# Second attention: score products of 128 rows, and the probabilities' low part right behind the logits

## The chip, the cores and the metric

The kernel runs on one core of a Trainium2 chip. The metric is the device time of one launch in microseconds (us). A profiled execution is read beside it: its span runs from the first to the last instruction. Engines: TensorE (PE, and PEld for its weight loads), VectorE (DVE), ScalarE (ACT), GpSimd (POOL), SyncE (SP, here the queue of the weight transfers).

## The reference

A bidirectional encoder trunk of two layers on 512 tokens of 1024 features, all float32. Layer 0 mixes tokens by 2-D neighbourhood attention, layer 1 by sliding-window attention; each is followed by a squared-ReLU MLP, each part is preceded by an RMS norm, and one closes the trunk. The change lies in layer 1's attention:

```python
def sliding_window_gqa(h, w_qkv, sinks, rel_table, w_o):
    # 16 query heads of 64, 4 key/value heads; window |i-j| <= 128, in blocks of 128 tokens
    s = jnp.einsum('bnqhgd,bnjhd->bhgnqj', q, kb).astype(jnp.float32)
    ...
    s = jnp.where(jnp.asarray(mask), s + bias, jnp.finfo(jnp.float32).min)
    m = jnp.maximum(jnp.max(s, axis=-1, keepdims=True), sink)
    p = jnp.exp(s - m)
    p = p / (jnp.sum(p, axis=-1, keepdims=True) + jnp.exp(sink - m))
    o = jnp.einsum('bhgnqj,bnjhd->bnqhgd', p.astype(v.dtype), vb).reshape(B, S, D)
    return jnp.einsum('bsd,de->bse', o, w_o)
```

q is scaled by 1/8 (64 to the power -1/2), kb and vb are the keys and values of the three neighbouring blocks.

## The kernel before

Every operand of a matmul is held in two parts of a short format (fp32r): a high part, which ScalarE rounds off, and a low part, the rest, which VectorE gets by a subtraction. A product a x b is then three matmuls, high x high, low x high and high x low (`product`, L398; lines L400 to L402 of the profile). The weights come as 180 chunks of 128x1024, one transfer of 512 KB each, issued by SyncE when the chunk before is split; ScalarE makes w_hi (L802) and VectorE w_lo (L1086).

All engines run queues of their own, written out by hand in program order, and meet at semaphores. Nothing reorders them: an instruction that waits holds up all that is behind it on its engine.

The second attention runs over eight pairs of heads, p = 0 to 7, each with four blocks of 128 queries, n = 0 to 3. A block of one pair is called a unit here. Blocks 0 and 3 see two key blocks (256 columns), blocks 1 and 2 see three (384); so the two heads of a unit have 4 or 6 tiles of 128x128 probabilities (512 or 768 columns). A unit goes through this chain:

- TensorE `sw_scores` (L692, products at L504): for each of the two heads a contraction over its 64 features. Head 0 has its features in partitions 0 to 63 and head 1 in 64 to 127, so `head_products` (L498) issues high x high, high x low and low x high in pairs of 64-row matmuls, six in all. They go to one PSUM tile, s_ps, which is free again when the logits are made.
- VectorE `sw_logits` (L1364, L1178): adds the bias, negates and takes the minimum, one custom instruction a head.
- ScalarE `sw_exp` (L991, L864): exponential and row sum, one a head.
- TensorE `sw_transpose` (L701, L708): the 4 or 6 tiles, into pt_ps.
- ScalarE `pt_high` (L867, L869), VectorE `pt_low` (L1133, L1135): the two parts of the transposed probabilities, pt_parts.
- TensorE `sw_values` (L712; L534, L538): the weighted values, into one of two banks of om_ps, one for blocks 0 and 1 (g = 0), one for blocks 2 and 3 (g = 1).
- VectorE `sw_o_sum` (L1381, with L1386, L1389, L1143, L1145): adds the parts and divides, once for two blocks. TensorE `transpose_o` (L544, L547) transposes the result, ScalarE `sw_o_high` (L1013, L1015) and VectorE `sw_o_low` (L1397, L1399) split it.

`sw_step` exists on each engine and covers one pair: four positions n. TensorE's position n holds: the transposes of unit n-1, one dense part (three products of 512 columns for the next pair's queries, or in the last two steps for the output projection), the scores of unit n+1, another dense part, the values of unit n-1. The dense parts make the next query tile: VectorE scales it (`scale_queries`, L1115), ScalarE rounds it (`tile_high`, L856) and VectorE makes its low part (`queries_low`, L1125). One weight chunk a step is split too. The full steps are pairs 1 to 6; the step of pair 0 has no outputs before it, the step of pair 7 no queries behind it.

ScalarE's position n holds: the first exponential of unit n, [an output's high part], the transposed probabilities' high part of unit n-1, the second exponential of n, and what else is due. VectorE's position n holds: the logits of unit n, then outputs and queries where due, then the low part of unit n-1.

Of the kernel before, what the change touches and what calls it, by code (L numbers as in the profile page):

```python
# [19 lines left out]
ALU = mybir.AluOpType  # L20
ACT = mybir.ActivationFunctionType

P = 128
# [76 lines left out]
def encoder(nc, xT, wstream, gains, rpb, sinks, rel_table, na_mask, onehot, out):  # L100
# [3 lines left out]
    with ExitStack() as ctx:  # L104
# [71 lines left out]
        x_prepared, h_split, sq_cleared = sem("x_prepared"), sem("h_split"), sem("sq_cleared")  # L176
        idle_made, h_low, first_hi = sem("idle_made"), sem("h_low"), sem("first_hi")
# [61 lines left out]
        na_probs = probs[:, 0:QT * ROWS * WC].rearrange("p (j n) -> p j n", j=QT)  # L239

# [60 lines left out]
        def _(pool):  # L301
# [83 lines left out]
            split_weights(CH_MLP0 + 2)  # L385
            with pool.Fori(1, PAIRS // 2) as i:
# [10 lines left out]
        def _(pe):  # L397
# [294 lines left out]
            def sw_scores(p, n):  # L692

                if n == 0:
                    pe.wait_ge(tile_split, (p + (TI_SW + 3)).v)
                pe.wait_ge(logits_made, sw_unit(p, n).v)
                kb, nb = SW_BLOCKS[n]
                head_products(lambda hh: s_ps[:, hh, 0:nb * P], (8 + p.odd, slice(P * n, P * (n + 1))),
                              (p.odd, slice(P * kb, P * (kb + nb)))).then_inc(scores_done, 1)
# [29 lines left out]
            def sw_step(m, before=True, last=None):  # L729
# [59 lines left out]
            early_part(CH_SWO, GR_SWO, HEADS, 12, 16)  # L789
# [6 lines left out]
        def _(act):  # L796
# [50 lines left out]
            def tile_high(g, e, dst, square=None, order=None):  # L847
# [8 lines left out]
                nc.scalar.copy(dst, src).then_inc(tile_hi, 1)  # L856

# [202 lines left out]
            tile_high(At(GR_SW), At(TI_SW), k_hi[:, 0, :])  # L1060
            split_weights(At(CH_SW + 3))
            split_weights(At(CH_SW + 4))
            tile_high(At(GR_SW + 2), At(TI_SW + 1), k_hi[:, 1, :])
# [3 lines left out]
            tile_high(At(GR_SW + 4), At(TI_SW + 2), u_hi[:, 8, :])  # L1067
# [523 lines left out]
```

## Time and profile before

| | us |
|---|---|
| median of 3 runs (1148.69 to 1149.16) | 1148.82 |
| profiled execution | 1148.75 |
| its span | 1147.1 |
| TensorE busy | 1136.0 (99%) |
| VectorE busy | 630.4 (55%) |
| ScalarE busy | 504.8 (44%) |
| GpSimd busy | 138.0 (12%) |

The second attention, from its first scores (623) to its last values (753), takes 130 us of the span. A matmul's row in a timeline gives its start and a modelled time until its result is through; matmuls are pipelined, so the difference between two starts is what one costs, and the time in the second column is longer than that. For the other engines too the next instruction can start a little before the one ahead has ended. "[0.28 <-DVE nmax L1178]" behind a row means that its engine was idle for 0.28 us ahead of it, until VectorE's instruction of that line and tile released it. "x6" is a number of instructions merged into a row.

### The profile page before, as it was taken

The numbers are of one execution on the slowest core, as the hardware profiler recorded it, in microseconds if no ns is written. First come the engines' busy times: TensorE is split into PE (matmuls) and PEld (weight loads), VectorE is DVE, ScalarE is ACT, GpSimd is POOL, SyncE is SP. The second block draws the span as 40 slices with busy tenths as digits, with TensorE's granted clock in tenths as the row PEclk, the third lists the DMA queues.
The fourth block names the chain that finished last, engine by engine and source line by source line (L and its number), as shares of the span: only waits on it lengthen the run. The fifth ranks groups of instructions, "written<-read, shape, count | busy, mean of one in ns | idle before, by whom it ended". The sixth has DMA issues, their size and how long they took to land.

```text
span 1147.1 us, 16682 instructions
## 1 busy us (share of the span) xinstructions
PE 1136.0 (99%) x5644; PEld 937.1 (82%) x5644; DVE 630.4 (55%) x1020; ACT 504.8 (44%) x908; POOL 138.0 (12%) x239
## 2 busy tenths in 40 slices
PE   9999999999999999999999999999999999999997
PEld 6888888888888888888887788888888888888886
DVE  7788887764442234444345778766444223444333
ACT  6777677553431223333334666645343122333221
POOL 6544341330000000000000322100000000000000
PEclk9999999999999999999999999999999999999998
DMA  6322331343223222322222212123322332232222
GB/s 225 97 89 92 91 91 55 96 120 105 91 92 102 100 91 92 107 94 90 93 91 92 51 53 59 52 74 95 107 91 92 100 102 92 91 107 95 91 92 92
DMA packets 34291, 106.98 MB, mean 93 GB/s; under 512 B 5760, under 2 KB 8096, under 8 KB 34256
## 3 DMA queue, kind: packets, MB, share of 16 engines
q1 hardware_dynamic: 29344, 98.61, 26.2%
q0 software_dynamic: 4768, 7.90, 2.9%
q8 instruction: 21, 0.34, 0.1%
q14 instruction: 14, 0.11, 0.0%
q10 hardware_dynamic: 144, 0.02, 0.0%
HBM read 103.84 MB, written 2.67 MB: 93 GB/s over the span
## 4 chain that ended last, share of the span: by engine, by line
PE 98%; DVE 1%; DMA 0%; ACT 0%; SPq 0%; issue 0%; DVEq 0%; ACTq 0%
PE acc L400 29%; PE acc L402 28%; PE acc L401 28%; PE s_ps L504 3%; PE om_ps L538 2%; PE pt_ps L708 2%; PE om_ps L562 1%; PE om_ps L534 1%; PE pt_ps L525 1%; PE om_ps L494 1%; PE s_ps L400 1%; PE s_ps L401 1%; PE s_ps L402 1%; DMA w_raw<-in_wstream 0%; PE om_ps L547 0%; DVE x_res L1304 0%
## 5 line engine op out<-in xcount | busy, mean ns | idle before, releaser
L802 ACT CAST w_hi<-w_raw 128x1024 fp32r<-128x1024 f32 x179 | 188.1, 1051 | 401.5 <-PE acc L402 395.1
L400 PE MATMUL acc<-h_hi,w_hi 128*128 128x512 f32 x792 | 318.4, 402 | 0.7 <-DVE w_lo L1086 0.7
L401 PE MATMUL acc<-h_lo,w_hi 128*128 128x512 f32 x792 | 308.9, 390 | 0.0
L402 PE MATMUL acc<-h_hi,w_lo 128*128 128x512 f32 x792 | 308.8, 390 | 0.0
L1086 DVE TENSOR_TENSOR w_lo<-w_raw,w_hi 128x1024 fp32r<-128x1024 f32 x177 | 217.9, 1231 | 143.7 <-ACT w_hi L802 143.0
L400 PE MATMUL acc<-u_hi,w_hi 128*128 128x512 f32 (+1 forms) x624 | 241.2, 387 | 0.0
L401 PE MATMUL acc<-u_lo,w_hi 128*128 128x512 f32 (+1 forms) x624 | 239.5, 384 | 0.0
L402 PE MATMUL acc<-u_hi,w_lo 128*128 128x512 f32 (+1 forms) x624 | 239.5, 384 | 0.0
L400 PEld LDWEIGHTS acc<-h_hi,w_hi 128*128 128x128 f32 x792 | 148.8, 188 | 37.5 <-issue 4.8
L402 PEld LDWEIGHTS acc<-h_hi,w_lo 128*128 128x128 f32 x792 | 148.7, 188 | 31.7
L401 PEld LDWEIGHTS acc<-h_lo,w_hi 128*128 128x128 f32 x792 | 149.1, 188 | 28.5 <-issue 0.7
L1115 DVE SCALAR_TENSOR_TENSOR scaled<-acc,rstd 128x512 f32<-128x512 f32 x90 | 61.9, 689 | 143.9 <-PE acc L402 142.4
L400 PEld LDWEIGHTS acc<-u_hi,w_hi 128*128 128x128 f32 x624 | 117.2, 188 | 24.1 <-issue 0.5
L402 PEld LDWEIGHTS acc<-u_hi,w_lo 128*128 128x128 f32 x624 | 117.2, 188 | 23.2
L401 PEld LDWEIGHTS acc<-u_lo,w_hi 128*128 128x128 f32 x624 | 117.3, 188 | 22.6
L348 POOL DMA_DIRECT2D bias_pairs<-t_shifted x64 | 32.8, 575 | 448.9 <-ACT esink L1007 428.4
L864 ACT ACTIVATE probs<-probs,nmax 128x256 f32<-128x256 f32 (+1 forms) x128 | 67.9, 532 | 35.3 <-DVE nmax L1178 35.3
L1260 DVE TENSOR_TENSOR x_res<-acc,x_res 128x512 f32 (+1 forms) x39 | 26.9, 690 | 99.5 <-PE acc L402 99.5
L1125 DVE TENSOR_TENSOR u_lo<-scaled,u_hi 128x512 f32 (+1 forms) x80 | 59.1, 738 | 13.9 <-ACT u_hi L856 13.9
L331 POOL TENSOR_TENSOR bias_masked<-bias_pairs,mask 128x256 f32<-128x256 f32 x64 | 52.3, 857 | 83.2 <-DVE nmax L1178 81.2
L856 ACT CAST u_hi<-scaled 128x512 f32 (+1 forms) x80 | 49.7, 621 | 7.2
L1135 DVE TENSOR_TENSOR pt_parts<-pt_ps,pt_parts 128x1024 fp32r<-128x1024 f32 (+2 forms) x48 | 45.8, 955 | 10.5 <-ACT pt_parts L869 10.3
(141 smaller groups left out, 1000.1 us busy)
## 6 DMA issues: line engine op xcount, KB each, us to landing
w_raw<-in_wstream SPq DMA_DIRECT2D x180, 512.0 KB, 3.3
bias_pairs<-rpb_reversed POOLq DMA_DIRECT2D x64, 62.0 KB, 2.4
bias_pairs<-t_shifted POOLq DMA_DIRECT2D x64, 48.0 KB, 2.2
x_res<-in_xT SPq DMA_DIRECT2D x8, 256.0 KB, 5.6
out_y<-x_res SPq DMA_DIRECT2D x8, 128.0 KB, 1.8
out_y<-x_res SPq DMA_DIRECT2D x4, 256.0 KB, 2.3
t_shifted<-vT POOLq DMA_DIRECT2D x16, 31.0 KB, 2.1
mask<-in_mask POOLq DMA_DIRECT2D x1, 64.0 KB, 5.5
```

What stands on the lines that cost most here:

```text
L331: ins = nc.gpsimd.tensor_tensor(bias_m[:, g, i, :, :].rearrange("p c r -> p r c"), rows[:, :, U0[j]:U0[j] + WC], mask[:, j:j + 1, :].to_br ...
L400: nc.tensor.matmul(dst, a[0], b[0], start=start, stop=False)
L401: nc.tensor.matmul(dst, a[0], b[1], start=False, stop=False)
L402: return nc.tensor.matmul(dst, a[1], b[0], start=False, stop=stop)
L504: ins = nc.tensor.matmul(dst(hh), a[s, queries[0], queries[1]], b[s, keys[0], keys[1]], start=start, stop=stop)
L802: nc.scalar.copy(w_hi[:, c.odd, :], w_raw[:, c.odd, :]).then_inc(w_hi_made, 1)
L856: nc.scalar.copy(dst, src).then_inc(tile_hi, 1)
L864: return nc.scalar.activation(src, src, ACT.Exp, bias=nmax[:, slot, i:i + 1], scale=-1.0, accum_out=rsum[:, slot, i:i + 1])
L1086: nc.vector.tensor_tensor(w_lo[:, c.odd, :], w_raw[:, c.odd, :], f32(w_hi[:, c.odd, :]), ALU.subtract).then_inc(w_split, 1)
L1115: nc.vector.scalar_tensor_tensor(out=dst, in0=order(bank), scalar=factor, in1=order(rstd[:]), op0=op, op1=ALU.mult).then_inc(acc_taken, 1)
L1125: nc.vector.tensor_tensor(order[0](dst), order[1](scaled[:, e.odd, :]), order[0](f32(hi)), ALU.subtract).then_inc(tile_split, 1)
L1135: nc.vector.tensor_tensor(pt_lo[:, 0:blocks, :], pt_ps[:, 0:blocks, :], f32(pt_hi[:, 0:blocks, :]), ALU.subtract).then_inc(pt_split, 1)
```

## The change

Scores. Each head's query stack gets 128 rows: its own 64 rows hold the high part and the other 64 the low part (`q_stack`: head 0 in u_hi, head 1 in u_lo). The keys' high part is held in both halves (`k_stack_hi`, in k_hi and k_lo), and so is their low part (`k_stack_lo`, in four spare tiles of u_hi). A head's scores are then two matmuls of 128 rows, with the four partial products instead of three. ScalarE makes the queries' high parts by two copies of 64x512 (`queries_high`) and the keys' by four a tile (`keys_high`), VectorE the low parts by two subtractions of 64x512 (`queries_low`, `keys_low`), and GpSimd copies the keys' low part into the other half, four copies in all, with a semaphore of its own.

Order. On VectorE the low part of unit n-1 stands right behind the logits of n; only an output's low part (at positions 1 and 3) stands between them. The sum of outputs, the scaled queries and their low part stand behind it, at positions 1 and 3, 1, and 2. On ScalarE the output's high part stands behind the second exponential. On TensorE the transposes of an output stand between the first dense part and the scores, at positions 0 and 2 of the next step.

```diff
@@ gpsimd, ahead of the loop over pairs @@
+            for kv in range(2):
+                pool.wait_ge(tile_split, TI_SW + kv + 1)
+                for hh in range(2):
+                    nc.gpsimd.tensor_copy(k_stack_lo(kv, hh)[HEAD_ROWS[1 - hh], :],
+                                          f32(k_stack_lo(kv, hh)[HEAD_ROWS[hh], :])).then_inc(keys_doubled, 1)
+                    pool.wait_ge(keys_doubled, 2 * kv + hh + 1)
@@ tensor, sw_scores @@
+                    pe.wait_ge(keys_doubled, 2 if p.a == 0 and p.b == 0 else 4)
                 pe.wait_ge(logits_made, sw_unit(p, n).v)
                 kb, nb = SW_BLOCKS[n]
-                head_products(lambda hh: s_ps[:, hh, 0:nb * P], (8 + p.odd, slice(P * n, P * (n + 1))),
-                              (p.odd, slice(P * kb, P * (kb + nb)))).then_inc(scores_done, 1)
+                for hh in range(2):
+                    queries, keys = q_stack(p.odd, hh)[:, P * n:P * (n + 1)], slice(P * kb, P * (kb + nb))
+                    nc.tensor.matmul(s_ps[:, hh, 0:nb * P], queries, k_stack_hi(p.odd, hh)[:, keys], start=True, stop=False)
+                    ins = nc.tensor.matmul(s_ps[:, hh, 0:nb * P], queries, k_stack_lo(p.odd, hh)[:, keys], start=False,
+                                           stop=True)
+                ins.then_inc(scores_done, 1)
@@ tensor, sw_step @@
                     dense_part(2 * n)
+                    if n == 0 and before:
+                        transpose_o(p * 2 + (HEADS - 2), sw_bank(0))
+                    if n == 2 and before:
+                        transpose_o(p * 2 + (HEADS - 1), sw_bank(1))
                     if n < 3 or last != 8:
                         sw_scores(*sw_unit_by(p, n, 1))
                     dense_part(2 * n + 1)
-                    if n == 1 and before:
-                        transpose_o(p * 2 + (HEADS - 1), sw_bank(1))
-                    if n == 3:
-                        transpose_o(p * 2 + HEADS, sw_bank(0))
@@ scalar @@
+            def queries_high(m):
+                act.wait_ge(acc_taken, (m + (GR_SW + 5)).v)
+                src = scaled[:, m.odd, :]
+                nc.scalar.copy(q_stack(m.odd, 0)[TOP, :], src[TOP, :])
+                nc.scalar.copy(q_stack(m.odd, 1)[BOTTOM, :], src[BOTTOM, :]).then_inc(tile_hi, 1)
@@ scalar, sw_step @@
                     sw_exp(p, n, 0)
-                    if n == 0 and before:
-                        sw_o_high(p + -1, 0)
-                    if n == 2 and before:
-                        sw_o_high(p + -1, 1)
                     if before or n >= 1:
                         sw_pt_high(*sw_unit_by(p, n, -1))
                     sw_exp(p, n, 1)
                     if n % 2 == 1:
                         sw_sinks(p, n // 2)
+                    if n == 0 and before:
+                        sw_o_high(p + -1, 0)
                     if n == 2 and dense:
-                        tile_high(m + (GR_SW + 4), m + (TI_SW + 2), u_hi[:, 8 + m.odd, :])
+                        queries_high(m)
+                    if n == 2 and before:
+                        sw_o_high(p + -1, 1)
@@ vector @@
             def queries_low(m):
-                tile_low(m + (TI_SW + 2), u_lo[:, 8 + m.odd, :], u_hi[:, 8 + m.odd, :])
+                dve.wait_ge(tile_hi, (m + (TI_SW + 3)).v)
+                for hh in range(2):
+                    own, other = HEAD_ROWS[hh], HEAD_ROWS[1 - hh]
+                    ins = nc.vector.tensor_tensor(q_stack(m.odd, hh)[other, :], scaled[own, m.odd, :],
+                                                  f32(q_stack(m.odd, hh)[own, :]), ALU.subtract)
+                ins.then_inc(tile_split, 1)
@@ vector, sw_step @@
                     sw_logits(p, n)
-                    if n == 0 and before:
+                    if n == 1 and before:
                         sw_o_low(p + -1, 0)
-                    if n == 1 and before:
-                        sw_o_sum(p + -1, 1)
-                    if n == 2 and before:
+                    if n == 3 and before:
                         sw_o_low(p + -1, 1)
-                    if n == 2 and dense:
-                        scale_queries(m)
-                    if n == 3 and dense:
-                        queries_low(m)
-                    if n == 3:
-                        sw_o_sum(p, 0)
                     if before or n >= 1:
                         sw_pt_low(*sw_unit_by(p, n, -1))
                     if n == 0:
                         split_weights(m + (CH_SW + 5))
+                    if n == 1 and before:
+                        sw_o_sum(p + -1, 1)
+                    if n == 1 and dense:
+                        scale_queries(m)
+                    if n == 2 and dense:
+                        queries_low(m)
+                    if n == 3:
+                        sw_o_sum(p, 0)
```

VectorE in the loop of the second attention, from the second half of the logits of unit 1 (384 columns) to the first logits of unit 2. Before (ISA rows are the custom instruction and its second result):

```order
L1178 ISA probs,nmax<-s_ps,bias_pairs,sw_nsink 128x384
L1178 ISA nmax 128x1
L1385 REGISTER_ALU
L1386 TENSOR_TENSOR rden<-rsum,esink 128x4
L1389 RECIPROCAL rden<-rden 128x4
L1143 TENSOR_REDUCE o_raw<-om_ps 128x256
L1144 REGISTER_ALU
L1145 TENSOR_TENSOR o_tok<-o_raw,rden 128x2x2x64
L1135 TENSOR_TENSOR pt_parts<-pt_ps,pt_parts 128x512
L1366 REGISTER_ALU
L1178 ISA probs,nmax<-s_ps,bias_pairs,sw_nsink 128x384
```

The same engine and place of the changed kernel, from the low part of the probabilities of unit 0 to the first logits of unit 2:

```order
L1179 TENSOR_TENSOR pt_parts<-pt_ps,pt_parts 128x512
L1429 REGISTER_ALU
L1430 TENSOR_TENSOR rden<-rsum,esink 128x4
L1433 RECIPROCAL rden<-rden 128x4
L1187 TENSOR_REDUCE o_raw<-om_ps 128x256
L1188 REGISTER_ALU
L1189 TENSOR_TENSOR o_tok<-o_raw,rden 128x2x2x64
L1164 REGISTER_ALU
L1158 REGISTER_ALU
L1159 SCALAR_TENSOR_TENSOR scaled<-acc,rstd 128x512
L1410 REGISTER_ALU
L1222 ISA probs,nmax<-s_ps,bias_pairs,sw_nsink 128x384
```

The low part (pt_parts) stood last ahead of the next logits; now the four instructions of the sum of outputs and the scaled queries stand between the two.

TensorE in the same loop, position 2, from the end of the first dense part to the start of the second, with the scores of unit 3 (256 columns). Before:

```order
L402 MATMUL acc<-h_hi,w_lo 128x512
L696 REGISTER_ALU
L504 MATMUL s_ps<-k_hi,u_hi 128x256 x2
L504 MATMUL s_ps<-k_lo,u_hi 128x256 x2
L504 MATMUL s_ps<-k_hi,u_lo 128x256 x2
L400 MATMUL acc<-h_hi,w_hi 128x512
```

The same place of the changed kernel:

```order
L423 MATMUL acc<-h_hi,w_lo 128x512
L566 REGISTER_ALU
L568 MATMUL om_ps<-ident,o_tok 128x128 x2
L718 REGISTER_ALU
L722 MATMUL s_ps<-k_hi,u_hi 128x256
L723 MATMUL s_ps<-u_hi 128x256
L722 MATMUL s_ps<-k_lo,u_lo 128x256
L723 MATMUL s_ps<-u_hi,u_lo 128x256
L421 MATMUL acc<-h_hi,w_hi 128x512
```

Six score matmuls became four, and the transposes of an output (om_ps<-ident,o_tok) came in ahead of them.

## Rows read from the trace of the kernel before

**Rows 1.** The page, part 4: chain that ended last, by engine

```profile
PE 98%; DVE 1%; DMA 0%; ACT 0%; SPq 0%; issue 0%; DVEq 0%; ACTq 0%
```

**Rows 2.** Stretches, one step: us, busy (instructions) by engine, clock, DMA

```profile
core 0: us, PE busy (x) PEld busy (x) DVE busy (x) ACT busy (x) POOL busy (x), PEclk, DMA share, GB/s
662.00:677.91 15.91, 15.91 (x115) 12.80 (x114) 12.88 (x33) 10.06 (x30) 4.34 (x10) 1.00 0.24 59
```

**Rows 3.** TensorE's waits, 600 to 775: us in total, times, longest

```profile
PE om_ps L538 <- DVE pt_parts L1135: 0.3, 1, 0.3
```

**Rows 4.** TensorE's timeline: start us, us, engine, line, instruction

```profile
667.27 0.39 PE L402 MATMUL acc<-h_hi,w_lo 128*128 128x512 f32 x1
667.59 0.39 PE L504 MATMUL s_ps<-k_hi,u_hi 64*128 64x256 f32 x2
667.81 0.28 PE L504 MATMUL s_ps<-k_lo,u_hi 64*128 64x256 f32 x2
667.93 0.28 PE L504 MATMUL s_ps<-k_hi,u_lo 64*128 64x256 f32 x2
668.14 0.50 PE L400 MATMUL acc<-h_hi,w_hi 128*128 128x512 f32 x1
668.48 0.40 PE L401 MATMUL acc<-h_lo,w_hi 128*128 128x512 f32 x1
668.72 0.40 PE L402 MATMUL acc<-h_hi,w_lo 128*128 128x512 f32 x1
```

**Rows 5.** TensorE's timeline, first attention, products of 256 columns on 128 rows

```profile
111.86 1.12 PE L562 MATMUL om_ps<-pt_parts,v_parts 128*128 128x256 f32 x8
112.82 1.03 PE L525 MATMUL pt_ps<-ident,probs 128*128 128x128 f32 x8
```

**Rows 6.** Tile om_ps: count, then ns min/median/max, first and last start

```profile
L1162 DVE TENSOR_TENSOR o_tok<-om_ps,o_raw x16: 397/410/429, 45.4 to 212.2; 64x256 f32<-64x256 f32 x16
```

**Rows 7.** VectorE's timeline in steps of the second attention

```profile
674.55 0.16 DVE L1386 TENSOR_TENSOR rden<-rsum,esink 128x4 f32<-128x4 f32 x1
...
675.68 0.42 DVE L1145 TENSOR_TENSOR o_tok<-o_raw,rden 128x256 f32<-128x256 f32 x1
676.02 0.68 DVE L1135 TENSOR_TENSOR pt_parts<-pt_ps,pt_parts 128x512 fp32r<-128x512 f32 x1
676.62 0.61 DVE L1178 CUSTOM_DVE_ANT_0 probs<-s_ps,bias_pairs,sw_nsink 128x384 f32<-128x384 f32 x1
...
679.62 0.96 DVE L1135 TENSOR_TENSOR pt_parts<-pt_ps,pt_parts 128x768 fp32r<-128x768 f32 x1 [0.20 <-ACT pt_parts L869]
680.50 0.48 DVE L1178 CUSTOM_DVE_ANT_0 probs<-s_ps,bias_pairs,sw_nsink 128x256 f32<-128x256 f32 x1
...
688.26 1.21 DVE L1086 TENSOR_TENSOR w_lo<-w_raw,w_hi 128x1024 fp32r<-128x1024 f32 x1
689.40 0.61 DVE L1178 CUSTOM_DVE_ANT_0 probs<-s_ps,bias_pairs,sw_nsink 128x384 f32<-128x384 f32 x1
```

**Rows 8.** ScalarE's timeline in the same stretch

```profile
677.27 0.62 ACT L864 ACTIVATE probs<-probs,nmax 128x384 f32<-128x384 f32 x1 [0.98 <-DVE nmax L1178]
...
678.79 0.80 ACT L869 CAST pt_parts<-pt_ps 128x768 fp32r<-128x768 f32 x1 [0.55 <-PE pt_ps L708]
679.49 0.62 ACT L864 ACTIVATE probs<-probs,nmax 128x384 f32<-128x384 f32 x1
...
680.10 0.61 ACT L856 CAST u_hi<-scaled 128x512 fp32r<-128x512 f32 x1
681.02 0.51 ACT L864 ACTIVATE probs<-probs,nmax 128x256 f32<-128x256 f32 x1 [0.31 <-DVE nmax L1178]
...
687.03 0.59 ACT L869 CAST pt_parts<-pt_ps 128x512 fp32r<-128x512 f32 x1 [0.76 <-PE pt_ps L708]
```

**Rows 9.** Timelines ahead of the first scores: ScalarE, VectorE, TensorE

```profile
621.02 0.61 ACT L856 CAST u_hi<-scaled 128x512 fp32r<-128x512 f32 x1
621.54 0.58 ACT L860 CAST v_parts<-om_ps 128x512 fp32r<-128x512 f32 x1
...
621.66 0.69 DVE L1125 TENSOR_TENSOR u_lo<-scaled,u_hi 128x512 fp32r<-128x512 f32 x1 [0.84 <-ACT u_hi L856]
622.27 0.68 DVE L1130 TENSOR_TENSOR v_parts<-om_ps,v_parts 128x512 fp32r<-128x512 f32 x1
...
623.16 0.38 PE L504 MATMUL s_ps<-k_hi,u_hi 64*128 64x256 f32 x2
```

**Rows 10.** The page, part 5: GpSimd's additions

```profile
L331 POOL TENSOR_TENSOR bias_masked<-bias_pairs,mask 128x256 f32<-128x256 f32 x64 | 52.3, 857 | 83.2 <-DVE nmax L1178 81.2
```

More of the change, by code:

```diff
@@ L176, in encoder @@
         x_prepared, h_split, sq_cleared = sem("x_prepared"), sem("h_split"), sem("sq_cleared")
+        keys_doubled = sem("keys_doubled")
         idle_made, h_low, first_hi = sem("idle_made"), sem("h_low"), sem("first_hi")
@@ L239, in encoder, with q_stack, k_stack_hi, k_stack_lo @@
         na_probs = probs[:, 0:QT * ROWS * WC].rearrange("p (j n) -> p j n", j=QT)
+        HEAD_ROWS = (TOP, BOTTOM)
+        def q_stack(odd, hh):
+            return (u_lo if hh else u_hi)[:, 8 + odd, :]
+        def k_stack_hi(kv, hh):
+            return (k_lo if hh else k_hi)[:, kv, :]
+        def k_stack_lo(kv, hh):
+            return u_hi[:, 10 + 2 * kv + hh, :]
         def sw_probs(n, hh):
@@ L788, in _ @@
             sw_transpose(At(7), 3)
-            early_part(CH_SWO, GR_SWO, HEADS, 12, 16)
+            early_part(CH_SWO, GR_SWO, HEADS, 12, 14)
+            transpose_o(At(2 * HEADS - 2), sw_bank(0))
+            early_part(CH_SWO, GR_SWO, HEADS, 14, 16)
             sw_values(At(7), 3)
@@ L856, in tile_high, with keys_high @@
                 nc.scalar.copy(dst, src).then_inc(tile_hi, 1)
+            def queries_high(m):
[3 more added lines that the diff above has]
+                nc.scalar.copy(q_stack(m.odd, 1)[BOTTOM, :], src[BOTTOM, :]).then_inc(tile_hi, 1)
+            def keys_high(kv):
+                act.wait_ge(acc_taken, GR_SW + 2 * kv + 1)
+                src = scaled[:, kv, :]
+                for hh in range(2):
+                    for half in HEAD_ROWS:
+                        ins = nc.scalar.copy(k_stack_hi(kv, hh)[half, :], src[HEAD_ROWS[hh], :])
+                ins.then_inc(tile_hi, 1)
             def v_high(batch, dst):
@@ L1059, in _ @@
             split_weights(At(CH_SW + 2))
-            tile_high(At(GR_SW), At(TI_SW), k_hi[:, 0, :])
+            keys_high(0)
             split_weights(At(CH_SW + 3))
             split_weights(At(CH_SW + 4))
-            tile_high(At(GR_SW + 2), At(TI_SW + 1), k_hi[:, 1, :])
+            keys_high(1)
             v_high(At(UNITS_NA), v_hi[:, 0:4, :, :])
@@ L1066, in _ @@
             split_weights(At(CH_SW + 6))
-            tile_high(At(GR_SW + 4), At(TI_SW + 2), u_hi[:, 8, :])
+            queries_high(At(0))
             v_high(At(UNITS_NA + 1), v_hi[:, 4:8, :, :])
@@ L1073, in _ @@
             sw_step(At(8), dense=False)
+            sw_pt_high(At(7), 3)
             sw_o_high(At(7), 0)
-            sw_pt_high(At(7), 3)
             split_weights(At(CH_SWO + 3))
@@ L1405, in queries_low, with keys_low @@
             def queries_low(m):
-                tile_low(m + (TI_SW + 2), u_lo[:, 8 + m.odd, :], u_hi[:, 8 + m.odd, :])
+                dve.wait_ge(tile_hi, (m + (TI_SW + 3)).v)
+                for hh in range(2):
+                    own, other = HEAD_ROWS[hh], HEAD_ROWS[1 - hh]
+                    ins = nc.vector.tensor_tensor(q_stack(m.odd, hh)[other, :], scaled[own, m.odd, :],
+                                                  f32(q_stack(m.odd, hh)[own, :]), ALU.subtract)
+                ins.then_inc(tile_split, 1)
+            def keys_low(kv):
+                dve.wait_ge(tile_hi, TI_SW + kv + 1)
+                for hh in range(2):
+                    own = HEAD_ROWS[hh]
+                    ins = nc.vector.tensor_tensor(k_stack_lo(kv, hh)[own, :], scaled[own, kv, :],
+                                                  f32(k_stack_hi(kv, hh)[own, :]), ALU.subtract)
+                ins.then_inc(tile_split, 1)
             def sw_step(m, before=True, dense=True):
@@ L1470, in _ @@
             split_weights(At(CH_SW + 2))
-            tile_low(At(TI_SW), k_lo[:, 0, :], k_hi[:, 0, :])
+            keys_low(0)
             dve.wait_ge(t5_stored, 16 * QC)
@@ L1476, in _ @@
             split_weights(At(CH_SW + 4))
-            tile_low(At(TI_SW + 1), k_lo[:, 1, :], k_hi[:, 1, :])
+            keys_low(1)
             v_low(At(UNITS_NA), slice(0, 4))
@@ L1489, in _ @@
             sw_step(At(8), dense=False)
+            sw_pt_low(At(7), 3)
             sw_o_low(At(7), 0)
-            sw_pt_low(At(7), 3)
             split_weights(At(CH_SWO + 3))
```

## The prediction

> **What bounds the kernel now.** I read the chain that ended last first: 98% of it is TensorE, so the whole program is a row of matmuls with almost no waits [rows 1]. The change touches only the second attention, so I cut its steady part into steps of one head pair with the table of stretches: 15.91 us a step, TensorE busy in all of it, VectorE busy 12.88 us, ScalarE 10.06 us, granted clock 1.00 (the upper of the two levels, 2.4 GHz) [rows 2]. The waits list has only 0.3 us of waiting for the probabilities' low part in the whole stage [rows 3]. TensorE sets the step, and VectorE has 3 us of room in it. The next question is whether that room is of the kind that the change needs, so I read the timelines of VectorE and ScalarE link by link.
>
> **Scores on TensorE (removed: 6 matmuls of 64 rows a unit, added: 4 of 128 rows).** In the timeline a unit of 256 columns is three pairs. The second and third pair start 0.12 us apart, so the two halves of a pair run side by side, in the time of one. But around them time is lost: from the start of the dense matmul ahead (667.27) to the start of the second dense matmul behind (668.48) are 1.21 us, of which two dense matmuls are worth 2 x 0.24 (668.48 to 668.72), so a unit costs 0.73 us, where three pairs at 0.12 would be 0.36 [rows 4]. The remaining 0.37 us stand at the two changes between 64 and 128 rows. Dense products of 256 columns on 128 rows are in the first attention: eight, start to start with what follows, take 112.82 - 111.86 = 0.96 us, 0.12 each [rows 5]. So four cost 0.48, and a unit saves 0.25 us. For 384 columns I scale the 0.12 to 0.18: three pairs against four passes, so 0.19 saved if the bubbles are the same. A step has two units of each: 2 x 0.25 + 2 x 0.19 = 0.9 us less TensorE work, a step of about 15.0; over eight steps 7 us. Bounds: if the dense products met bubbles of the same 0.37 us, a unit would cost 0.85 or 1.09 and the step be 0.6 us longer (16.5); if they ran without any, as the 0.96 us row says, 15.0. I take 15.0, that row being the same shape. The transposes of an attention output only change places, at the same count.
>
> The Trainium skill, TensorEngine Tiling (Array Packing), section "When to Use Tiling", names a contraction of at most 64 as the case for two row tiles, which is what the change gives up; by that alone four passes replace three, and 32 units would cost 4 to 6 us more (worked from the 0.12 and 0.18 above). The same page's "Key Properties" says that changing the tiling mode drains TensorE. This trace has both: pairs side by side, and 0.37 us at the changes [rows 4], and the second outweighs the first.
>
> **VectorE and ScalarE (added work).** Each of the seven later query tiles is now rounded by two ScalarE copies of 64x512 instead of one of 128x512, and its low part made by two VectorE subtractions instead of one. Half the partitions are not cheaper: VectorE's 64x256 additions took 0.41 us, its 128x256 multiplication 0.42 [rows 6, 7]. So half-height instructions cost what full-height ones do: 0.52 us more on ScalarE, start to start, and 0.61 more on VectorE [rows 9]. VectorE's work in a step becomes about 13.5 us. As a sum this still fits in 15.0.
>
> **The order (moved).** It does not fit as a chain. ScalarE's queue in a position is: first exponential of unit n, then the high part of the transposed probabilities of unit n-1, then the second exponential of n. VectorE's low part of n-1 can't begin before that high part, which stands behind the exponential, which needs VectorE's logits of n. Before, VectorE's other work (the sum of outputs, the scaled queries) stood between the logits and the low part: it ran while ScalarE did its two links. Now it stands behind the low part and ahead of the next logits: VectorE idles during ScalarE's links, and ScalarE waits during VectorE's extras. One round through the two engines, link by link [rows 7, 8]:
> - logits to first exponential: 0.65 us for 384 columns (676.62 to 677.27), 0.52 for 256 (680.50 to 681.02)
> - exponential 0.62 or 0.51; high part to low part 0.83 for 768 columns (678.79 to 679.62), 0.62 for 512 (its 0.59 and the same 0.03)
> - low part 0.88 (679.62 to 680.50) or 0.60 (676.02 to 676.62)
> - extras: sum of outputs with its denominators 1.47 (674.55 to 676.02), weight split 1.14 (688.26 to 689.40), scaled queries 0.61 (as the subtraction, [rows 9])
>
> Position 1 of a step: 0.65 + 0.62 + 0.62 + 0.60 + 1.47 + 0.61 = 4.57. Position 2: the queries' low part waits for ScalarE's copies, which stand behind the high part (0.70, 678.79 to 679.49) and the second exponential (0.61): 0.65 + 0.62 + 0.70 + 0.61 + 0.52 + 0.64 + 2 x 0.61 = 4.96. Position 3: 0.52 + 0.51 + 0.83 + 0.88 + 1.47 = 4.21. Position 0: 0.52 + 0.51 + 0.62 + 0.60 + 1.14 = 3.39. Sum 17.13 us a step, against 15.91 now and 15.0 that TensorE needs: the pair VectorE and ScalarE becomes the bound, at +1.22 us a step. TensorE would wait about 2.1 us a step, in pieces: at the values for the low part of units 1 and 2 and at the scores of unit 3, which need the bank of unit 2's logits, now behind the sum and the scaling.
>
> The same sum for the old order shows that it is no artefact: there position 1 has the sum of outputs (1.47) beside exponential and high part (1.24), so the round is two logits (2 x 0.61 at most) + 1.47 + 0.60 = 3.3 us, below a quarter of TensorE's step (4.0).
>
> The full round is in the six steps of the loop (pairs 1 to 6): 6 x 1.22 = 7.3 us. In the first step there are no outputs of an earlier pair to sum, in the last no queries: there I take gain and stall as even, 0 (bounds -0.9 and +1.2 each).
>
> **Before the first step.** The first scores start at 623.16. They need the values' low part, which stands behind the queries' low part on VectorE and behind its copy on ScalarE. The copies would end at 621.02 + 0.52 + 0.61 = 622.15, the two subtractions (0.03 later, 0.61 each) at 623.40, the values' low part (0.68) at 624.08 [rows 9]. That is 1.0 us after 623.16 (0 if something hid it, at most 1.2). The keys' four copies and GpSimd's doubling of the low parts come 10 us earlier, in a stretch where both engines idle for 3 us at a time; nothing here shows GpSimd's 64x512 copy, so I bound it by the 128x256 additions that are there, 0.86 us each [rows 10], and by four times that, 3.4 us: still in time. Cost 0. GpSimd's later bias loads queue behind it and are not due for 20 us.
>
> **Sum.** +7.3 +1.0 = +8.3 us. The profiled execution took 1148.75 us, the median is 1148.82, so they are one: 1157.1, I say 1157.0. After this stage the program is TensorE alone, and nothing gives the time back.
>
> **Rivals.**
> - *TensorE stays the bound* (faster). For it: TensorE is 98% of the chain, VectorE's sum of work fits. Against it: the round above is built of links that the old trace shows one by one. It decides at 15.9: a round below that gives a faster kernel, and one under 15.0, 2.1 us less than mine, all of the saving. Then 7 us less and 1 lost at the start: 1148.75 - 7 + 1 = 1143.
> - *The queries' second halves hardly count.* If the 64-row instructions on disjoint halves cost half, or their wait is hidden, position 2 loses 0.52 + 0.61 = 1.13 us and the round is 16.0, the old step: 1149 to 1152 with the start. Against it is the 0.41 us of a half-height subtraction, but none of exactly this kind is in the trace.
> - *It is slower through TensorE itself:* the dense products pay the drains too and the clock falls in the new waits. The chip granted 1.00 through the stage, with one wait of 0.3 us; I expect waits of 0.5 to 0.8 us, ten times as many. If it fell to 1.2 GHz for a quarter of the stage (130 us), 16 us or more would come on top: 1170.
> - *The scores' change has no effect because the hardware does not save the bubbles.* This changes nothing in my forecast, since 16.5 is below 17.13; it tells only in the first rival.
>
> **How the numbers follow.** Forecast (the round binds) 0.73; queries cheap 0.13, half of which within 0.2%; TensorE bound 0.11; clock 0.03. 0.2% (2.3 us) is what a measurement tells from no change here. Slower: 0.73 + 0.06 + 0.03 = 0.82; same 0.07; faster 0.11. Range: the round's bounds are 16.0 and, with 0.1 us more at each position, 17.5. The low end is 6 x 0.09 + 1.0 - 0.9 above 1148.8, so 1149.5; the high end 6 x 1.6 + 1.0 + 1.2, so 1160.5. The first rival stays outside.
>
> **What would show it.** Right: step of about 17 us in the stage; on TensorE waits for pt_parts at the values, and for nmax at the scores, together 2 us a step; VectorE idle 3.5 us a step, released by ScalarE's pt_parts cast and the queries' cast, with ScalarE idle released by VectorE's logits; score products 0.12 us apart with no gap at either end; the first scores near 624.1. Wrong: no waits on TensorE and a step near 15, or a step of 17 with TensorE busy in all of it. The tail after the stage should be the old one, moved.

## The result and the profile after

The changed kernel takes 1161.95 us (median of 5 runs, 1161.70 to 1163.43), the kernel before 1148.82: slower, ratio 1.0117 with a 95% interval of 1.0103 to 1.0130. The spans are 1160.0 and 1147.1 us, 12.9 us apart. The forecast had the direction, and 8 of the 13 us; the time lies outside its range.

The chain that ended last is no longer TensorE alone (page, part 4; before: [rows 1]):

```profile
PE 88%; DVE 4%; ACT 4%; issue 3%; DMA 0%; DVEq 0%; ACTq 0%
```

TensorE's waits in the second attention (600 to 790; before: [rows 3]). Columns: us in total, times, longest.

```profile
PE om_ps L559 <- DVE pt_parts L1179: 7.1, 16, 0.5
PE s_ps L722 <- DVE nmax L1222: 4.3, 14, 0.5
PE s_ps L722 <- DVE v_parts L1174: 1.2, 1, 1.2
```

TensorE waits at the values for the low part and at the scores for the logits, as forecast. In the six full steps below it is 12 times each, 5.4 and 3.5 us: two waits of each kind a step. The forecast had two at the values and one at the scores; the scores of the next pair's first unit wait too. By this list that is 1.5 us of waiting a step, forecast 2.1; a wait also delays the products behind it (last section), so the step grows by more. The third row is the start of the stage.

The six full steps, cut at the transposes of unit 1 (us, busy and instructions by engine, clock, DMA; before: [rows 2]):

```profile
647.89:665.40 17.51, 16.00 (x107) 13.50 (x106) 13.77 (x36) 10.59 (x29) 4.35 (x10) 1.00 0.18 53
665.40:683.30 17.90, 16.44 (x106) 13.34 (x106) 13.73 (x34) 10.60 (x29) 4.36 (x10) 1.00 0.19 52
683.30:700.80 17.50, 15.99 (x107) 13.47 (x106) 13.76 (x36) 10.60 (x29) 4.35 (x10) 1.00 0.17 52
700.80:718.71 17.91, 16.46 (x107) 13.39 (x106) 13.74 (x34) 10.59 (x29) 4.35 (x10) 1.00 0.19 53
718.71:736.23 17.52, 16.00 (x106) 13.54 (x106) 13.78 (x35) 10.60 (x29) 4.36 (x10) 1.00 0.17 52
736.23:753.67 17.44, 15.98 (x106) 13.50 (x106) 13.71 (x35) 10.59 (x29) 0.00 (x0) 1.00 0.10 32
```

17.63 us a step on average, where the forecast had 17.13 and the kernel before 15.92. The clock is 1.00 all through, so no part of this is TensorE's clock. Two of the six steps are 0.4 longer.

VectorE over one round, with the second instruction of each logits pair left out:

```profile
679.73 0.61 DVE L1222 CUSTOM_DVE_ANT_0 probs<-s_ps,bias_pairs,sw_nsink 128x384 f32<-128x384 f32 x1
...
681.61 0.69 DVE L1179 TENSOR_TENSOR pt_parts<-pt_ps,pt_parts 128x512 fp32r<-128x512 f32 x1 [0.38 <-ACT pt_parts L913]
...
684.28 0.61 DVE L1222 CUSTOM_DVE_ANT_0 probs<-s_ps,bias_pairs,sw_nsink 128x384 f32<-128x384 f32 x1
...
686.35 0.96 DVE L1179 TENSOR_TENSOR pt_parts<-pt_ps,pt_parts 128x768 fp32r<-128x768 f32 x1 [0.92 <-ACT pt_parts L913]
688.10 0.69 DVE L1453 TENSOR_TENSOR u_hi<-scaled,u_hi 64x512 fp32r<-64x512 f32 x1 [0.79 <-ACT u_lo L891]
688.80 0.69 DVE L1453 TENSOR_TENSOR u_lo<-scaled,u_lo 64x512 fp32r<-64x512 f32 x1
689.52 0.48 DVE L1222 CUSTOM_DVE_ANT_0 probs<-s_ps,bias_pairs,sw_nsink 128x256 f32<-128x256 f32 x1
...
693.82 0.48 DVE L1222 CUSTOM_DVE_ANT_0 probs<-s_ps,bias_pairs,sw_nsink 128x256 f32<-128x256 f32 x1
...
697.19 0.61 DVE L1222 CUSTOM_DVE_ANT_0 probs<-s_ps,bias_pairs,sw_nsink 128x384 f32<-128x384 f32 x1
```

From logits to logits the four positions 1, 2, 3, 0 take 4.55, 5.24, 4.30 and 3.37 us. The forecast had 4.57, 4.96, 4.21 and 3.39. VectorE is idle wherever ScalarE's cast is due (0.38, 0.92, 0.79), and ScalarE in turn for the logits (2.38 us). Its reads of the accumulator, two rows, are left out here:

```profile
684.93 0.61 ACT L908 ACTIVATE probs<-probs,nmax 128x384 f32<-128x384 f32 x1 [2.38 <-DVE nmax L1222]
685.54 0.78 ACT L913 CAST pt_parts<-pt_ps 128x768 fp32r<-128x768 f32 x1
686.22 0.62 ACT L908 ACTIVATE probs<-probs,nmax 128x384 f32<-128x384 f32 x1
686.83 0.60 ACT L890 CAST u_hi<-scaled 64x512 fp32r<-64x512 f32 x1
687.45 0.62 ACT L891 CAST u_lo<-scaled 64x512 fp32r<-64x512 f32 x1
688.09 0.37 ACT L1059 CAST u_hi<-om_ps 128x256 f32 x1
```

That is the round: neither engine is full, each waits for the other in turn.

Where the 12.9 us are, from the start of the first scores (S), of the transposes of unit 1 (T, pair in brackets) and of the last values (V) in TensorE's timelines:

| stretch | before | after | more | forecast |
|---|---|---|---|---|
| up to S | 623.16 | 624.36 | 1.2 | 1.0 |
| S to T (1) | 22.87 | 23.53 | 0.7 | 0 |
| T (1) to T (7), six steps | 95.63 | 105.78 | 10.15 | 7.3 |
| T (7) to V (7) | 11.48 | 12.41 | 0.9 | 0 |

Together 12.9, the whole difference: nothing comes before the stage or behind it.

### The profile page after: what moved, and what is told of

Same layout as the page of the kernel before. It is cut to its first block, busy times and chain, and to the rows that moved or that the text cites. A ratio compares the mean times of both kernels' runs of the same rounds, so it can differ in the third digit from the quotient of the medians.

```text
span 1160.0 us, 16589 instructions
## 1 busy us (share of the span) xinstructions
PE 1136.2 (98%) x5580; PEld 941.5 (81%) x5580; DVE 639.2 (55%) x1030; ACT 512.7 (44%) x922; POOL 141.2 (12%) x243
## 4 chain that ended last, share of the span: by engine, by line
PE 88%; DVE 4%; ACT 4%; issue 3%; DMA 0%; DVEq 0%; ACTq 0%
PE acc L421 27%; PE acc L422 26%; PE acc L423 26%; PE om_ps L583 1%; PE s_ps L525 1%; PE pt_ps L546 1%; DVE probs L1222 1%; ACT probs L908 1%; ACT pt_parts L913 1%; PE om_ps L515 1%; PE s_ps L421 1%; PE s_ps L422 1%; PE s_ps L423 1%; DVE o_raw L1187 1%; DVE pt_parts L1179 1%
## 5 line engine op out<-in xcount | busy, mean ns | idle before, releaser
L1169 DVE TENSOR_TENSOR u_lo<-scaled,u_hi 128x512 f32 (+1 forms) x72 | 53.6, 744 | 13.1 <-ACT u_hi L884 13.1
L840 ACT ACTIVATE h_hi<-x_res,gain 128x512 fp32r<-128x512 f32 (+1 forms) x24 | 17.4, 723 | 69.5 <-DVE x_res L1304 61.1
L884 ACT CAST u_hi<-scaled 128x512 f32 (+1 forms) x72 | 44.8, 623 | 7.2
```

Of the source, the lines that this page charges most:

```text
L1169: nc.vector.tensor_tensor(order[0](dst), order[1](scaled[:, e.odd, :]), order[0](f32(hi)), ALU.subtract).then_inc(tile_split, 1)
```

## The experiments

Theory A: the order makes a round through VectorE and ScalarE the bound. Theory B: the added instructions cost the time, in whatever order. Times are medians; "change" is against the kernel before, run beside it (1148.7 to 1149.0).

| kernel | us | change | 95% interval of the ratio | step, us |
|---|---|---|---|---|
| new instructions, old order | 1150.96 | +2.2 | 1.0011 to 1.0030 | 16.06 |
| old instructions, new order | 1154.21 | +5.4 | 1.0031 to 1.0064 | 16.5, 16.9 |
| high part first | 1151.74 | +2.9 | 1.0016 to 1.0036 | 16.05, 16.27 |
| both engines reordered | 1146.01 | -2.8 | 0.9968 to 0.9987 | 15.28, 15.50 |
| that order, old instructions | 1149.12 | +0.2 | 0.9993 to 1.0012 | 15.93 |
| queries in one | 1154.43 | +5.5 | 1.0030 to 1.0063 | 16.62, 16.86 |
| full height, twice | 1159.32 | +10.6 | 1.0077 to 1.0107 | 17.2, 17.6 |
| loops written out | 1159.84 | +10.9 | 1.0077 to 1.0111 | 17.33 |
| reordered, start untied | 1145.43 | -3.5 | 0.9955 to 0.9980 | 15.27, 15.50 |
| the same, loops written out | 1144.92 | -3.8 | 0.9955 to 0.9979 | 15.28 |

**New instructions, old order.** The change's stacks, casts, subtractions and products; `sw_step` and the tail of the stage as before on all engines.

```diff
-                    if n == 0 and before:
-                        transpose_o(p * 2 + (HEADS - 2), sw_bank(0))
...
+                    if n == 3:
+                        transpose_o(p * 2 + HEADS, sw_bank(0))
...
+                    if n == 2 and dense:
+                        scale_queries(m)
+                    if n == 3 and dense:
+                        queries_low(m)
+                    if n == 3:
+                        sw_o_sum(p, 0)
                     if before or n >= 1:
                         sw_pt_low(*sw_unit_by(p, n, -1))
...
-                    if n == 1 and dense:
-                        scale_queries(m)
-                    if n == 2 and dense:
-                        queries_low(m)
-                    if n == 3:
-                        sw_o_sum(p, 0)
```

> The change's score products, stacks and half-height instructions, in the order of the kernel before on all engines. Theory A (the order makes a round through VectorE and ScalarE the bound; the new instructions alone cost little because the old order hides them behind each other): 15.8 us a step and 1.2 us later at the start, 1148 us. Theory B (the added half-height casts and subtractions and the dense products themselves cost the 13 us, in whatever order): 1158 to 1162. If TensorE alone counted (6 to 7 us less work, start 1.2 later): 1143.

1150.96. Theory B's 1158 to 1162 is out: the same instructions cost 2 us here and 13 in the new order. But A's 1148 is missed too: 3 us dearer, a step of 16.06 where 15.8 was expected. The products are what they were forecast to be. TensorE's timeline, a unit of 256 columns:

```profile
664.64 0.40 PE L423 MATMUL acc<-h_hi,w_lo 128*128 128x512 f32 x1
664.88 0.27 PE L722 MATMUL s_ps<-k_hi,u_hi 128*128 128x256 f32 x1
664.99 0.28 PE L723 MATMUL s_ps<-u_hi 128*128 128x256 f32 x1
665.11 0.28 PE L722 MATMUL s_ps<-k_lo,u_lo 128*128 128x256 f32 x1
665.23 0.28 PE L723 MATMUL s_ps<-u_hi,u_lo 128*128 128x256 f32 x1
665.35 0.40 PE L421 MATMUL acc<-h_hi,w_hi 128*128 128x512 f32 x1
665.58 0.40 PE L422 MATMUL acc<-h_lo,w_hi 128*128 128x512 f32 x1
```

From 664.64 to 665.58 are 0.94 us, against 1.21 in [rows 4]: 0.27 saved, forecast 0.25. No gap stands at either end. What they save is lost again in waits. The waits list of this kernel for TensorE, 600 to 790, and the longest row of the one for its weight loads:

```profile
PE om_ps L559 <- DVE pt_parts L1177: 2.7, 8, 0.4
PE s_ps L722 <- DVE v_parts L1172: 1.2, 1, 1.2
PE s_ps L722 <- DVE nmax L1220: 0.5, 1, 0.5
PEld om_ps L559 <- DVE pt_parts L1177: 9.0, 21, 0.6
```

With TensorE's slot shorter, the low part comes too late. The longest wait is at position 3, where the values start 0.74 us behind the transposes of an output instead of 0.14:

```profile
670.16 0.38 PE L568 MATMUL om_ps<-ident,o_tok 128*128 128x128 f32 x2
670.90 0.33 PE L559 MATMUL om_ps<-v_parts,pt_parts 128*128 128x128 f32 x1 [0.36 <-DVE pt_parts L1177]
```

At positions 2 and 1 the values come 0.28 and about 0.2 us late in the same way, together some 1.1 us a step, a little more than the 0.9 that the products save. In the old order too a faster TensorE runs into the chain.

**Old instructions, new order.** The kernel before, with the order of the change in `sw_step` of the three engines and at the stage's tail (the hunks of the change that move lines, and none that replaces instructions).

> The kernel before with the change's order on all engines, old score products and full-height queries. Theory A: the round without the second cast and subtraction is 16.4 to 16.8 us against 15.9, so 4 us over the stage, 1153 us. Theory B: no change, 1148.8.

1154.21, 1.2 above A's figure; B's 1148.8 is out. The order costs 5.4 us by itself, the instructions by themselves 2.2, and together they cost 13.1: 5.5 us arise only where both meet. "Queries in one" below splits them.

**High part first.** The changed kernel with two lines exchanged on ScalarE:

```diff
-                    sw_exp(p, n, 0)
                     if before or n >= 1:
                         sw_pt_high(*sw_unit_by(p, n, -1))
+                    sw_exp(p, n, 0)
                     sw_exp(p, n, 1)
```

> The changed kernel with ScalarE's high part of the transposed probabilities ahead of the first exponential in each position, nothing else. Theory A: the link logits to exponential to high part leaves the round, which falls to about 16.1 us a step: 1152 us. Theory B (amount of work, not its chain): no change, 1162.

1151.74, 10.2 us less than the changed kernel, and not an instruction was taken away. This is the sharpest proof of the round, because the exchange removes just one link: the cast no longer stands behind an exponential that needs the next logits.

**Both engines reordered.** High part first, and on VectorE:

```diff
+                    if n == 2 and dense:
+                        scale_queries(m)
+                    if n == 3 and dense:
+                        queries_low(m)
                     if n == 3 and before:
                         sw_o_low(p + -1, 1)
                     if before or n >= 1:
                         sw_pt_low(*sw_unit_by(p, n, -1))
+                    if n == 1 and before:
+                        sw_o_sum(p + -1, 1)
                     if n == 0:
                         split_weights(m + (CH_SW + 5))
-                    if n == 1 and before:
-                        sw_o_sum(p + -1, 1)
-                    if n == 1 and dense:
-                        scale_queries(m)
-                    if n == 2 and dense:
-                        queries_low(m)
```

> As e4, and on VectorE the scaled queries go to position 2 and the queries' low part to position 3, both ahead of the probabilities' low part, so that they fill its wait. Theory A: round below TensorE's work, 15.3 us a step, start still 1.2 later: 1146 us, 2 to 3 us below the kernel before. Theory B: 1162.

1146.01, faster than both kernels. Beside the exchange on ScalarE, only the queries move: VectorE scales them and makes their low part one position later, ahead of the probabilities' low part, in the gap in which it waited for ScalarE's cast. The sums of outputs stay behind that low part, as in the change (at position 1 no weight split is due, so their two places in the cut are the same one). In the six steps (646.60 to 738.76) nothing is left on TensorE's own waits list; the largest that stay are those of its weight loads:

```profile
PEld om_ps L559 <- DVE pt_parts L1179: 3.2, 12, 0.4
PEld s_ps L722 <- issue: 1.3, 4, 0.3
```

**That order, old instructions.** The kernel before with the good order.

```diff
# against the kernel before, ScalarE; VectorE and TensorE as in "both engines reordered"
-                    sw_exp(p, n, 0)
                     if before or n >= 1:
                         sw_pt_high(*sw_unit_by(p, n, -1))
+                    sw_exp(p, n, 0)
```

> The kernel before with the good order of the reordered kernel, but the old six score products of 64 rows and full-height queries. It tells what the dense products are worth where TensorE is the bound. If they save 0.25 and 0.19 us a unit as predicted, 6 to 7 us of TensorE work, less 1.2 at the start: this one 1151 or more. If they save about 0.13 a unit (4 us): 1148.8, the time of the kernel before. If they save nothing: 1145.

1149.12, no different from the kernel before, so the middle case: the good order alone brings nothing where TensorE was the bound already. The dense products bring 3.1 us (1149.12 to 1146.01), although the first scores come 1.5 us later (624.49 for 622.98): a step falls from 15.93 to 15.28 or 15.50. That is 0.4 to 0.65 us a step, not the 0.9 that four units are worth; the rest is in the short waits above. In the 15.50 us from 661.88 in the reordered kernel's trace I find matmuls starting late at four places: 0.06 us at the values of position 2, 0.16 at the scores and 0.10 at the values of position 3, 0.20 at the scores of position 0. Without these 0.5 us the step would be 15.0, the forecast's figure for TensorE.

**Queries in one.** Against the changed kernel (the stacks hold high parts in one tile and low parts in the other, so the scores are other sums than the reference's):

```diff
-                nc.scalar.copy(q_stack(m.odd, 0)[TOP, :], src[TOP, :])
-                nc.scalar.copy(q_stack(m.odd, 1)[BOTTOM, :], src[BOTTOM, :]).then_inc(tile_hi, 1)
+                nc.scalar.copy(q_stack(m.odd, 0), src).then_inc(tile_hi, 1)
...
+                nc.vector.tensor_tensor(q_stack(m.odd, 1), scaled[:, m.odd, :], f32(q_stack(m.odd, 0)),
+                                        ALU.subtract).then_inc(tile_split, 1)
```

> The changed kernel, its order kept, with each later query tile rounded by one 128x512 cast and its low part made by one 128x512 subtraction (the stacks then hold high parts in one tile and low parts in the other, so the scores are other sums than the reference's). Theory A: 1.26 us of casts become 0.61 and 1.42 us of subtractions 0.61 in position 2 of the round, 1.1 to 1.2 us a step for six or seven steps, and 0.9 at the start: 1153 to 1154 us. If the half-height instructions were off the round: 1162.

1154.43: 7.5 us less than the changed kernel, 0.94 of them at the start (first scores at 623.42). Over the six full steps it is 5.3 us, 0.9 a step, for one cast and one subtraction less. Rival 2 of the prediction, that they hardly count, is out. VectorE's position 2 falls by 1.44 us, from 5.24 to 3.80, but position 3 rises from 4.30 to 4.85, because a third engine enters the round there: ScalarE's cast now waits for TensorE's transposes, and the low part for the cast.

```profile
668.92 0.80 ACT L912 CAST pt_parts<-pt_ps 128x768 fp32r<-128x768 f32 x1 [0.43 <-PE pt_ps L734]
669.75 0.96 DVE L1178 TENSOR_TENSOR pt_parts<-pt_ps,pt_parts 128x768 fp32r<-128x768 f32 x1 [1.16 <-ACT pt_parts L912]
```

So the links of VectorE and ScalarE alone, which rival 2 added up to 16.0 us a step, would have been too short: this kernel takes 16.7. Beside "old instructions, new order" (1154.21) it also splits the loss. The two differ in the score products and the keys' preparation, and take the same time within 0.2 us: where the round binds, the dense products gain nothing. The 13.1 us are 5.4 for the order, 0.2 for the dense products and 7.5 for the added cast and subtraction.

**Full height, twice.** Against the changed kernel, over all 128 partitions (other values in the stacks again):

```diff
-                nc.scalar.copy(q_stack(m.odd, 0)[TOP, :], src[TOP, :])
-                nc.scalar.copy(q_stack(m.odd, 1)[BOTTOM, :], src[BOTTOM, :]).then_inc(tile_hi, 1)
+                nc.scalar.copy(q_stack(m.odd, 0), src)
+                nc.scalar.copy(q_stack(m.odd, 1), src).then_inc(tile_hi, 1)
...
-                    ins = nc.vector.tensor_tensor(q_stack(m.odd, hh)[other, :], scaled[own, m.odd, :],
-                                                  f32(q_stack(m.odd, hh)[own, :]), ALU.subtract)
+                    ins = nc.vector.tensor_tensor(q_stack(m.odd, hh), scaled[:, m.odd, :],
+                                                  f32(q_stack(m.odd, hh)), ALU.subtract)
```

> The changed kernel, order kept, with the two casts and the two subtractions of each later query tile over all 128 partitions instead of 64 each (same counts and columns; the stacks then hold other values, so the scores are other sums). In the changed kernel the half-height subtractions start 0.70 us apart and the casts 0.62, where full-height ones elsewhere start 0.61 and 0.52 apart. Theory C (an instruction on the other half of the partitions doesn't overlap the one before): the overlaps come back, some 0.3 us a step, about 2 us less, 1160. Theory D (operands written and read in place, or whatever stands behind, set these distances): 1162.

1159.32, 2.6 us less with twice the elements. The timelines show that the overlaps come back: 0.61 us between the starts of the subtractions and 0.50 between those of the casts. VectorE's position 2 takes 4.92 us instead of 5.24.

```profile
687.00 0.69 DVE L1452 TENSOR_TENSOR u_hi<-scaled,u_hi 128x512 fp32r<-128x512 f32 x1 [0.68 <-ACT u_lo L891]
687.61 0.68 DVE L1452 TENSOR_TENSOR u_lo<-scaled,u_lo 128x512 fp32r<-128x512 f32 x1
688.22 0.48 DVE L1222 CUSTOM_DVE_ANT_0 probs<-s_ps,bias_pairs,sw_nsink 128x256 f32<-128x256 f32 x1
```

```profile
685.85 0.61 ACT L890 CAST u_hi<-scaled 128x512 fp32r<-128x512 f32 x1
686.35 0.62 ACT L891 CAST u_lo<-scaled 128x512 fp32r<-128x512 f32 x1
```

The durations are the same as at half height (0.69, 0.61); only the overlap with the neighbours differs. Theory D is out: the operands are still in place, and the same rows stand behind.

**Loops written out.** Against the changed kernel, on VectorE and ScalarE:

```diff
-            with dve.Fori(0, 3) as i:
-                for n in range(2):
-                    sw_step(At(2 + n, 2, i))
+            for step in range(2, 8):
+                sw_step(At(step))
```

> The changed kernel with VectorE's and ScalarE's loop over the steps of the second attention written out (pairs 1 to 6), TensorE's kept. The trace after shows 0.5 us in front of the logits of every second step with nothing to wait for. If that is the loop's jump: two or three of them go, 0.9 to 1.3 us less, 1160.7 to 1161.1. If it is something else in that place: 1162.

1159.84: 2.1 us less, more than expected, and all steps alike at 17.33. The loop has three turns of two steps; in the changed kernel the gap stands in two of the six steps, with nothing to wait for:

```profile
675.41 0.43 DVE L1189 TENSOR_TENSOR o_tok<-o_raw,rden 128x256 f32<-128x256 f32 x1
676.36 0.48 DVE L1222 CUSTOM_DVE_ANT_0 probs<-s_ps,bias_pairs,sw_nsink 128x256 f32<-128x256 f32 x1 [0.52 <-issue]
```

Written out it is gone:

```profile
674.96 0.43 DVE L1188 TENSOR_TENSOR o_tok<-o_raw,rden 128x256 f32<-128x256 f32 x1
675.30 0.48 DVE L1221 CUSTOM_DVE_ANT_0 probs<-s_ps,bias_pairs,sw_nsink 128x256 f32<-128x256 f32 x1
```

That is 0.95 us from the multiplication to the next pair's logits with the jump and 0.34 without, and it is position 3 of the round: 4.79 us with the jump, 4.30 in the other steps, 4.19 in all steps written out. So the two jumps make up 1.2 of the 2.1 us. The other steps lose about 0.1 at the same place; I take that for the register instructions that a written-out step does without, but no run isolates it.

**Reordered, start untied.** Against "both engines reordered":

```diff
-            pe.wait_ge(v_split, UNITS_NA + 2)
             sw_scores(At(0), 0)
+            pe.wait_ge(v_split, UNITS_NA + 2)
```

> The reordered kernel, and TensorE's wait for the values' low part stands behind the first scores instead of ahead of them. The first scores then wait for the queries' low part alone, 0.7 us earlier: 1145.3 if the logits behind them can use it, 1146.0 if ScalarE's loading of its function table or the next wait takes it up.

1145.43. The first scores start at 623.89 instead of 624.49, and the 0.6 us are kept to the end.

**The same, loops written out.** TensorE's loop too.

> The reordered kernel with the untied start, and the loops over the steps of the second attention written out on TensorE, VectorE and ScalarE. There TensorE is the bound in most of the step, and every second step is 0.2 us longer: if that is the loop's jump on the other two engines reaching TensorE, 0.4 to 0.8 us less than 1145.4, so 1144.8. If only TensorE's own jump counts or none: 1145.4.

1144.92, at the expected figure, but 0.5 us is about what such a comparison resolves. It is the best version here: 3.8 us below the kernel before, 17 below the change.

## Why the prediction was wrong, point by point

- **The bound: right.** The rounds that were added up link by link give 4.57, 3.39 and 4.21 for three positions that took 4.55, 3.37 and, without the loop's jump, 4.30. VectorE idles 3.4 us a step for ScalarE's casts, forecast 3.5. Two lines exchanged on ScalarE gave back 10.2 us of 13.1.
- **The half-height instructions: the step that failed in size.** "So half-height instructions cost what full-height ones do: 0.52 us more on ScalarE, start to start, and 0.61 more on VectorE." Their durations do, but the next instruction doesn't overlap them: 0.62 us start to start on ScalarE, 0.70 and 0.72 on VectorE. Position 2 took 5.24 instead of 4.96, 0.28 us more in each of six steps. With full-height pairs it is 4.92, so this is all of that position's miss. The rows that I used ([rows 6]) give durations, and the distance between two half-height additions, which is in the same trace, I didn't look at: those of the first attention start 0.43 us apart and last 0.42, no overlap either.
- **The loop's jump: missing.** It is not in the sum at all. Position 3 took 4.79 us in the two steps with the jump and 4.30 in the others, forecast 4.21; written out it takes 4.19. In the kernel before, all steps take 15.92 to 15.96 us, so TensorE as the bound hid it.
- **The first and last steps: taken at 0, measured 0.7 and 0.9.** Positions 2 and 3 stall in them as in the others (0.42 and 0.41 us at the values in the first, 0.45 and 0.47 in the last, in TensorE's timeline), and behind the last cut only one unit's scores are left to save on. The gain was taken to even out the stall, without a row for it; the upper bounds of 1.2 each held them.
- **The start: right,** 1.2 for 1.0 (its own links, 623.16 to 624.08, give 0.9); the subtractions there stand 0.70 and 0.72 apart too. GpSimd's copies cost nothing, as forecast: each pair took 2.3 us or less, and the last ended at 614.9.
- **TensorE's saving: right, and without effect in the change.** 0.27 for 0.25 a unit of 256 columns. The Trainium skill's drain at a change of tiling mode (TensorEngine Tiling (Array Packing), "Key Properties") agrees with what went, 0.37 us a unit in [rows 4]: the gaps at both ends vanish with the 64-row products. The rule of the same page of the Trainium skill ("When to Use Tiling") to use row tiles for contractions up to 64 would lose here: the dense products are 3.1 us faster in the good order, start included.
- **Sum of the miss:** in the six steps 10.15 less 7.3, 2.9 us (position 2: 6 x 0.28 = 1.7; position 3 with the loop: 6 x 0.09 and 2 x 0.49 = 1.5; positions 0 and 1 and rounding take 0.3 off), first and last step 1.6, start 0.2: 4.7, and 8.3 + 4.7 is the 12.9 of the spans within 0.1.
- **The range** allowed 0.1 us more at each position, which makes 9.6 us for the six steps at its high end; they took 10.15, because both misses of the round fell where nothing was allowed for them. It also took the 1.2 us of the first and last steps once, though it had bounded each at 1.2; together they took 1.6.
- **The rivals:** TensorE as the bound (faster), cheap queries, and a falling clock are all out; the granted clock stayed at 1.00.

## What to carry to other kernels

Two engines that hand work to each other in turn need more than room in their sums: add the links of one full round, and compare it with the slot of the engine that is the bound. In a queue that runs in order, put work that nobody awaits into the gap where its engine would wait for the other, and the awaited instruction first in the other's queue; behind the awaited one, the same work lengthens every round. When a change makes the old bound give way, costs that it had hidden (loop jumps, lost overlaps) all appear at once, so leave room upwards for them.

## What the hardware showed that I had not expected

- Casts and subtractions on alternating halves of the partitions don't overlap: 64x512 instructions start 0.62 us (ScalarE) and 0.70 (VectorE) apart, 128x512 ones 0.50 and 0.61, at the same durations of 0.61 and 0.69. The same holds for a full-height instruction behind one on the other half: 0.64 us from the second cast to the output's cast, 0.72 from the second subtraction to the logits. But a half-height addition behind a full-height subtraction, both starting at partition 0, does overlap (trace after, first attention: 1.20 us long, the next starts after 1.10). So it may be the change of the starting partition, or the half height of the one ahead; no run separates them.
- A loop's jump on VectorE leaves it idle for 0.5 us between two instructions (0.52 us, "issue"). Where another engine is the bound it costs nothing: in "that order, old instructions" the same idle time stands twice in the six steps, 0.8 us together, and they all take 15.93 or 15.94 us.
- A short wait of TensorE costs more than its length. In the reordered kernel the scores at position 3 start 0.29 us behind the last dense product, 0.06 more than without a wait, and the second product then 0.22 behind the first instead of 0.12:

```profile
667.16 0.40 PE L423 MATMUL acc<-h_hi,w_lo 128*128 128x512 f32 x1
667.45 0.38 PE L722 MATMUL s_ps<-k_hi,u_hi 128*128 128x256 f32 x1
667.67 0.28 PE L723 MATMUL s_ps<-u_hi 128*128 128x256 f32 x1
667.79 0.28 PE L722 MATMUL s_ps<-k_lo,u_lo 128*128 128x256 f32 x1
```

0.06 us of waiting became 0.16. The weights of the first product were not loaded ahead here: their load starts at 667.45 with it, while in "new instructions, old order", without a wait, it starts at 668.77 and the product at 669.00.
